# Stick-breaking attention: where ScalarE copies the first key's score row

## The reference

```
def stick_breaking_block(q, k, v, q_pos, k_pos):
    z = einsum('bthd,bshd->bhts', q, k) * (SB_HEAD_DIM ** -0.5)
    mask = k_pos[None, :] < q_pos[:, None]
    log_fail = where(mask, log_sigmoid(-z), 0.0)
    after = cumsum(log_fail, axis=3, reverse=True) - log_fail
    a = where(mask, exp(log_sigmoid(z) + after), 0.0)
    return einsum('bhts,bshd->bthd', a, v)
```

## Time and profile before

| | value |
|---|---|
| median of three runs | 1090.89 us |
| profiled execution | 1091.26 us, span of its instructions 1089.4 us |
| granted TensorE clock | 0.995 of full speed over the span |
| attention part of pass 0, from its first Exp | 74.72 to 164.69, 89.97 us |
| attention part of passes 1, 2, 3 | 87.90, 87.89, 87.90 us |
| between two attention parts | 73.94 us each |
| in one attention part (pass 1) | PE 86.02, PEld 69.22, DVE 70.44, ACT 70.86 us busy |

### The profile page before, as it was taken

How to read it: one execution, slowest core, us unless ns; L and a number is a source line. 1 busy time by engine, 2 the same in 40 slices (tenths; PEclk the granted TensorE clock), 3 DMA queues, 4 the chain that set the end, 5 groups by cost and what they waited for, 6 DMA issues and landing times.

```text
span 1089.4 us, 16617 instructions
## 1 busy us (share of the span) xinstructions
PE 1064.0 (98%) x6260; PEld 974.8 (89%) x6260; DVE 650.7 (60%) x1139; ACT 571.7 (52%) x1264; POOL 133.6 (12%) x145
## 2 busy tenths in 40 slices
PE   8999999999999999999999999999999999999995
PEld 5998779998779998779998779999999999999994
DVE  6677798387798377797387797335522231362117
ACT  4557884467883467883567884554022123252221
POOL 0001102011112011012011012001200110121220
PEclk9999999999999999999999999999999999999997
DMA  8041032132031132031142140153111111111144
GB/s 295 1 130 49 20 109 63 57 97 96 20 127 50 62 96 86 23 136 40 61 112 70 39 135 24 40 187 109 39 39 39 40 45 52 39 40 40 39 193 174
DMA packets 41487, 84.86 MB, mean 78 GB/s; under 512 B 2112, under 2 KB 22208, under 8 KB 41280
## 3 DMA queue, kind: packets, MB, share of 16 engines
q1 hardware_dynamic: 40832, 81.43, 22.9%
q10 hardware_dynamic: 576, 2.36, 0.6%
HBM read 67.27 MB, written 16.52 MB: 77 GB/s over the span
## 4 chain that ended last, share of the span: by engine, by line
PE 78%; ACT 9%; DVE 9%; issue 3%; DMA 1%; ACTq 0%; POOL 0%; DVEq 0%; SPq 0%; POOLq 0%
PE bank L671 50%; PE bank L1012 9%; DVE E L1676 3%; PE bank L808 3%; ACT E L1298 2%; ACT SPH L1310 2%; PE bank L838 2%; ACT E L1293 2%; DVE E L1680 1%; PE bank L794 1%; PE bank L681 1%; PE bank L708 1%; PE bank L912 1%; PE bank L954 1%; PE bank L976 1%
## 5 line engine op out<-in xcount | busy, mean ns | idle before, releaser
L671 PE MATMUL bank<-xh,wh 128*128 128x384 f32 x1296 | 438.8, 339 | 3.1 <-issue 2.8
L671 PE MATMUL bank<-xh,wl 128*128 128x384 f32 x1296 | 439.8, 339 | 0.0
L671 PE MATMUL bank<-xl,wh 128*128 128x384 f32 x1296 | 439.2, 339 | 0.0
L671 PEld LDWEIGHTS bank<-xh,wh 128*128 128x128 f32 x1296 | 243.6, 188 | 11.2 <-issue 9.3
L671 PEld LDWEIGHTS bank<-xh,wl 128*128 128x128 f32 x1296 | 243.6, 188 | 4.5 <-issue 2.0
L671 PEld LDWEIGHTS bank<-xl,wh 128*128 128x128 f32 x1296 | 243.5, 188 | 3.2 <-issue 0.2
L1183 ACT ACTIVATE slot<-bank,ngate 128x384 f32<-128x384 f32 x48 | 27.7, 576 | 177.9 <-PE bank L671 175.3
L1450 DVE CAST wh<-wr 128x1024 fp32r<-128x1024 f32 x64 | 43.7, 683 | 99.0 <-PE bank L671 98.1
L1455 DVE TENSOR_TENSOR wl<-wr,wh 128x1024 fp32r<-128x1024 f32 x64 | 90.8, 1419 | 1.9
L1676 DVE SCALAR_TENSOR_TENSOR E<-E,bank 128x512 f32<-128x512 f32 (+3 forms) x96 | 53.1, 553 | 47.7 <-ACT E L1298 47.6
L1858 DVE TENSOR_TENSOR slot<-bank,slot 128x384 f32<-128x384 f32 x24 | 13.4, 556 | 96.6 <-PE bank L1012 96.6
(11 more groups left out here) (226 smaller groups left out, 1687.0 us busy)
## 6 DMA issues: line engine op xcount, KB each, us to landing
wr<-wch SPq DMA_DIRECT2D x64, 512.0 KB, 3.6
KTc<-ckT SPq DMA_DIRECT2D x4, 2048.0 KB, 9.6
Vc<-cv SPq DMA_DIRECT2D x4, 2048.0 KB, 8.3
graw<-gated SPq DMA_DIRECT2D x8, 576.0 KB, 7.7
xres<-xT SPq DMA_DIRECT2D x1, 4608.0 KB, 15.7
yT<-yb SPq DMA_DIRECT2D x6, 576.0 KB, 3.0
xw<-xT SPq DMA_DIRECT2D x4, 768.0 KB, 11.6
okT<-kT ACTq DMA_DIRECT2D x4, 576.0 KB, 3.0
```

Source lines behind the costliest of these rows:

```text
L671: i = nc.tensor.matmul(CH[n % 2][:, 0:WIN], weights[:, k, :], rows[:, k, w * WIN:(w + 1) * WIN], start=(m == 0), stop=(m == 23))
```

## The change

The row copy leaves its place between Exp and Ln and is issued in the same step behind the high part, in front of the RT row of tile n-2. There it waits for the step's softplus (`s_sp`), in steps of rank 0 too, where ScalarE did not wait for VectorE before. It now counts up a new semaphore, and TensorE waits for that before it adds to the bank that the copy reads. The number of instructions that compute is the same, and no DMA is touched.

```
@@ semaphores
+        s_zr = sem("first_key_row_copied")
@@ TensorE, before it adds to the score bank of tile m = n-2
                         if q == 0:
                             pe.wait_ge(s_cr, 3)
                             pe.wait_ge(s_sp, t + 1)
+                            pe.wait_ge(s_zr, SUMS * p + sums_until(m))
                             i = add(negtri, E[m % 2], c0)
                         else:
                             pe.wait_ge(s_sph, SPLITS * p + rows_until(m))
+                            pe.wait_ge(s_zr, SUMS * p + sums_until(m))
                             add(negtri_r[:, :], SPH[m % 2], c0)
@@ ScalarE, step n
                         nc.scalar.activation(E[n % 2][:, c0:QW], ZB[n % 4][:, c0:QW], ACT.Exp).then_inc(s_E, 1)
-                        if STEPS[n][1] > 0:
-                            need(act, s_Sl, SUMS * p + (sums_until(n - 4) if n >= 4 else 0))
-                            nc.scalar.activation(zr[n % 4][0:1, row_col(n):QW], ZB[n % 4][0:1, row_col(n):QW], ACT.Copy)
                         act.wait_ge(s_E, t + 1)
...
                         nc.scalar.activation(SPH[n % 2][:, c0:QW], E[n % 2][:, c0:QW], ACT.Copy).then_inc(s_sph, 1)
+                    if n < NS and STEPS[n][1] > 0:
+                        act.wait_ge(s_sp, NS * p + n + 1)
+                        need(act, s_Sl, SUMS * p + (sums_until(n - 4) if n >= 4 else 0))
+                        nc.scalar.activation(zr[n % 4][0:1, row_col(n):QW], ZB[n % 4][0:1, row_col(n):QW], ACT.Copy).then_inc(s_zr, 1)
```

## The result

The changed kernel takes 1099.13 us (median of six runs, 1097.50 to 1099.42), the kernel before 1091.42 in the same comparison (six runs, 1090.44 to 1092.22): ratio 1.0069, 95% interval 1.0056 to 1.0082. It is slower by 7.7 us, where 8.5 were predicted. The profiled execution took 1099.08 us for a span of 1097.3, before 1091.26 for 1089.4. Every time in this document is of runs at a granted TensorE clock of 0.993 or more; one run of the kernel that moves the rank-0 copies alone, at 0.652, took 1489.56 us and is left out of its median.

A forecast was written before the change was run, and what follows sets the result against it. It took ScalarE and VectorE to pace each pass to about step 18, TensorE the rest. Step terms of 2.18 us less 0.06 gave 2.12 per pass, 8.5 over four passes, so 1099.4 us; range 1095 to 1103.

The forecast's parts named there:

- The first part: Each attention pass to about step 18: paced by the ScalarE-VectorE loop, so a longer ScalarE step lengthens the pass one for one.
- The masked steps: Masked steps that copy lose the overlap of Exp and next instruction: 0.13 us at 256 columns, 0.12 at 384 and 512.
- Step 4 behind the low weights: Step 4's clip waits for VectorE's low weights, not Ln, so it gains little: 0.18 us more besides the lost overlap.
- Steps 8 and 9: Copy of step 8 waits for its mask and holds back the next Exp: 0.76 us more per pass by step 10.
- Unmasked steps: Steps 16 to 18, 512 columns: RT's 0.12 us wait for VectorE's difference takes the lost overlap, so 0.
- steps 0 and 1: Start of a pass: the copy waits for the masked softplus, but step 2's Exp waits for TensorE anyway: 0, at most 0.76.
- the new waits: TensorE's waits for the copy before adding to the bank: 0 taken, bound 0.48 us for the first of three matmuls.
- The exit from the first part: Behind step 19's low weights TensorE takes over; low row 0.06 us earlier, so 2.12 of 2.18 us per pass remains.
- Steps 19 to 21: After step 18: +0.30 us in step 19, about +0.15 in 20 and 21, hidden by TensorE; 0 taken, 0.45 other end.
- The sum: Whole kernel: 2.12 us per pass, 8.5 us over four passes, giving 1099.4 us.
- the 0.09 estimated from its 93 ns: Alternative estimate from the skill's SBUF latency: lost overlap 0.09 us per step, sum about 1.3 us lower.

The follow-up runs named there:

- the last kernel: Against the kernel before: copy put between clip and high part in steps 2, 3, 5, 10, 11, 12, 14, 15 only; 1086.11 us, ratio 0.9952.

## Why the prediction was right

- **The first part is paced by ScalarE and VectorE, and their delay passes on.** Shown: doubling the copy moved that part by the 8.8 us that it cost there, and putting the copy into idle time gained. (An Exp waited for TensorE nine times and not eight: once for the scores themselves, 1.7 us before step 1 of pass 0. Nothing hangs on it.)
- **The masked steps lose the overlap.** Measured per step of pass 1, after less before: 0.09, 0.08, 0.00 and 0.06 at 256 columns (predicted 0.13 each), 0.16, 0.16 and 0.10 in steps 5, 12 and 13 (0.12), 0.16 and 0.17 in steps 14 and 15 (0.12). In sum 0.98 for 1.12, and that is two errors with opposite signs, so the closeness is in part luck. At 384 and 512 columns the loss is larger, because the high part does not come forward by as much as Ln does: in step 14 by 0.31 us (2.65 to 2.34) and not 0.35, in step 5 by 0.22 and not 0.25. Step 7 of the kernel before already had it, with Ln 0.60 us and the high part 2.33 behind its Exp:

```profile
259.91 0.63 ACT L1310 ACTIVATE SPH<-E 128x512 fp32r<-128x512 f32 x1 [0.72 <-DVE E L1680]
```

At 256 columns the loss is smaller, because the prediction had no wait behind the high part in any masked step, and read that from one of 512 columns. In step 10 before, RT starts 0.09 us after the difference ends (266.64), just as in the unmasked step 16 of the earlier trace rows, and 0.40 behind the high part; the copy, which doesn't need the difference, starts 0.33 behind it. So 0.07 us of RT's place was a wait, and it takes that much of the 0.13:

```profile
266.23 0.41 DVE L1517 TENSOR_TENSOR zr<-bank,zr 1x256 f32<-1x256 f32 x1
266.33 0.42 ACT L1310 ACTIVATE SPH<-E 128x256 fp32r<-128x256 f32 x1 [0.71 <-DVE E L1680]
266.73 0.42 ACT L1315 ACTIVATE RT<-zr 1x256 fp32r<-1x256 f32 x1
```

Step 10's 0.00 hides another 0.06: at its end ScalarE had waited for TensorE's sum, and that wait is gone, as in the kernel that moves the rank-0 copies alone, where the step takes 3.02 instead of 3.08.

- **Step 4 behind the low weights.** Predicted 0.12+0.18 = 0.30, measured 0.30 (3.06 to 3.36); the clip comes 0.08 earlier relative to its Exp, for 0.07 predicted.
- **Steps 8 and 9.** Predicted 0.76, measured 0.76 (3.66 to 4.42), and shown by taking it out. The reason was the right one: the queue and not the copy. That the sum fits to 0.01 us is luck: the Exp of step 9 comes 0.99 us late and not 1.07, and step 9 takes 0.08 longer than counted.
- **Unmasked steps, steps 0 and 1, the new waits.** 0 predicted; 0.02, -0.01 and 0 measured. For steps 0 and 1 that held by about 0.2 us, as the doubled copy shows.
- **The exit from the first part.** Predicted 2.12 per pass, measured 2.01 in pass 1; pass to pass 1.67, 2.00 and 2.02. Pass 0 has 0.3 less: its step 13 took 3.76 us before, 3.51 or 3.52 in the others, and 3.63 after, so the unexplained 0.25 us that it had before went with the change. Steps 19 to 21 grew by 0.31 us, for 0.45 predicted, and were covered.
- **The sum.** The first three passes are 5.7 us longer. The first Exp of the run is 0.2 earlier and what follows the last pass's Exp 23 is as long as before (451.68 and 451.63 us), so the last pass's 2.38 to Exp 23 stays: 5.7+2.4-0.2 = 7.9, the difference of the spans. In that last stretch the 0.4 that TensorE covers was given back where the gated rows are loaded again at the end of pass 3, a transfer that took 5.75 us against 5.29. It is not a cost of the change: the same transfer took 5.27 in the kernel that leaves the rank-0 copies and 5.80 in the one that moves only those of steps 16 to 18. So 7.9 for 8.5 is the 0.56 too much for the masked steps, 0.3 less in pass 0, 0.2 less before the first Exp and 0.4 more in the last pass; the last three nearly cancel by luck.

The Trainium skill, "Perfetto Trace Analysis", section "Identifying the Most-Contended Engine", takes the engine with the highest share to be optimized first. That is TensorE, with 89% of the span in weight loads in both kernels. Here an edit on an engine that is busy for half of the span moved the time by 0.7% one way and, in another place, 0.5% the other. The same page of the Trainium skill, section "Optimizing Scalar/DVE Operations", which has half of the latency overlap the next instruction, agrees in sign: the overlap that the moved copy filled was lost. The loss measured was 0.10 to 0.17 us a step at 384 and 512 columns, above the 0.09 estimated from its 93 ns.

## What to carry to other kernels

Removing an instruction from between two dependent ones gives back less than its time (0.35 us of 0.48 here), since it overlapped the end of the first. When a piece is moved within a strict queue, look for where that queue stands still, not for what stops depending on it: here idle time lay 0.7 us wide in front of the high part, and the copy was put behind it; put into it, the same instruction made the kernel 0.4 to 0.5% faster. Look, too, at each size of step for itself: the wait that a following instruction has at 256 columns is not there at 512. And a wait that is harmless in most steps can stall the ones that were free of it, so the few steps of another kind are to be counted by themselves.

## What the runs showed of the hardware

A copy of one row takes as long as an Exp over 128 rows of the same length (0.57 us at 512 columns). A ScalarE copy from partition 0 to partition 32 took 0.59 instead of 0.57 us, but cost the queue 0.72, because it overlapped with neither the instruction before it nor the one behind; the same copy to partition 0 overlapped with both and cost 0.48. That it is the change of partition was not separated from the second write into the same tile.

Single steps are 0.25 to 0.3 us longer in one pass than in the others. In step 13 of pass 0 in the kernel before (3.76 us) no wait is shown for it. In step 1 of pass 1 in both kernels that move copies of late steps only, and of pass 2 in the last kernel (3.42 to 3.44, else 3.15), ScalarE waits that much longer for TensorE (1.63 to 1.65 us, before 1.36). They come and go with small changes of the program in places that the change doesn't touch, so a difference of 0.3 us in one pass of one profile says nothing; a difference that stands in four passes does.
